# Pair pipelines for the softmax attentions of a three-block transformer kernel: order of heads, product blocks and side work

## What is computed

```python
# first block: attentions
oa = softmax(qa @ ka.T * scale + rel_bias, causal) @ va          # 8 heads of 64
ob = stick_breaking(qb, kb, vb)                                  # 8 heads of 64
mixed = (g_a * (oa @ w_br_moba) + g_b * (ob @ w_br_sb)) @ w_out
# even block
w = p[:, :, 0] - lam * p[:, :, 1]; o_a = rmsnorm(w @ a_v, subln) * 0.8
idx = top_k(sum_h relu(i_q @ i_k.T) * i_w, 64)                   # per query
o_b = softmax over the selected keys (b_q @ b_k.T) @ b_v
x = x + rmsnorm(concat(o_a, o_b) @ even_w_out, g[3])
# odd block: two groups of 8 heads
o = softmax(q @ k.T * scale + bias, chunks <= own) @ v
x = x + rmsnorm(o @ odd_w_out, g[3])
```

## Time and profile before

| | us |
|---|---|
| median of three runs | 1498.01 (1497.97 to 1501.21) |
| the profiled execution | 1496.0 |
| its span | 1494.2 |
| PE busy in the span | 1420.8 |
| DVE busy | 894.2 |
| ACT busy | 748.2 |

### The profile page before, as it was taken

How to read it: one execution, slowest core, us unless ns; L and a number is a source line. 1 busy time by engine, 2 the same in 40 slices (tenths; PEclk the granted TensorE clock), 3 DMA queues, 4 the chain that set the end, 5 groups by cost and what they waited for, 6 DMA issues and landing times.

```text
span 1494.2 us, 18003 instructions
## 1 busy us (share of the span) xinstructions
PE 1420.8 (95%) x6775; PEld 1167.7 (78%) x6775; DVE 894.2 (60%) x1125; ACT 748.2 (50%) x1039; POOL 82.6 (6%) x133
## 2 busy tenths in 40 slices
PE   5999998999999999998799999999999999999998
PEld 4878877778877888876577888878888778778886
DVE  5577775788775554467746655456544454665543
ACT  4557735646545434355466543445344466564442
POOL 3011100000000000031200000000000100000000
PEclk9999999999999999999799999999999999999999
DMA  9787644467553766444224855638565363465650
GB/s 355 272 301 232 204 150 163 160 235 251 199 169 121 234 195 197 146 141 143 69 85 155 281 175 192 193 104 267 184 194 177 132 209 113 133 221 198 195 169 29
DMA packets 177446, 274.29 MB, mean 184 GB/s; under 512 B 6449, under 2 KB 120881, under 8 KB 177361
## 3 DMA queue, kind: packets, MB, share of 16 engines
q1 hardware_dynamic: 170656, 250.87, 50.8%
q0 software_dynamic: 5552, 20.20, 4.3%
q10 hardware_dynamic: 1153, 2.07, 0.4%
HBM read 272.05 MB, written 1.06 MB: 183 GB/s over the span
## 4 chain that ended last, share of the span: by engine, by line
PE 68%; DVE 8%; issue 3%; ACT 3%; DMA 1%; POOL 0%; DVEq 0%; SPq 0%; POOLq 0%; ACTq 0%
PE psum L2212 21%; PE psum L2214 21%; PE psum L2213 21%; DVE w_lo L1839 2%; PE psum L2413 2%; DVE PR L2151 1%; DMA raw<-in_w_up_dram 1%; ACT w_hi L1637 1%; DVE scr L2174 1%; PE psum L2288 1%; ACT attn L1757 0%; PE psum L2342 0%; PE psum L2341 0%; PE psum L2357 0%; DVE lo_qk L1839 0%
## 5 line engine op out<-in xcount | busy, mean ns | idle before, releaser
L1839 DVE TENSOR_TENSOR w_lo<-raw,w_hi 128x2048 fp32r<-128x2048 f32 (+1 forms) x158 | 358.6, 2273 | 213.0 <-ACT w_hi L1637 212.6
L2212 PE MATMUL psum<-w_hi,hT_hi 128*128 128x512 f32 x1000 | 400.9, 401 | 19.7 <-DVE w_lo L1839 8.5
L2214 PE MATMUL psum<-w_hi,hT_lo 128*128 128x512 f32 x1000 | 392.0, 392 | 0.0
L2213 PE MATMUL psum<-w_lo,hT_hi 128*128 128x512 f32 x1000 | 391.1, 391 | 0.0
L1637 ACT ACTIVATE w_hi<-raw 128x2048 fp32r<-128x2048 f32 (+1 forms) x158 | 300.0, 1901 | 136.6 <-PE psum L2214 92.4
L2212 PEld LDWEIGHTS psum<-w_hi,hT_hi 128*128 128x128 f32 x1000 | 189.6, 190 | 64.8 <-issue 17.5
L2214 PEld LDWEIGHTS psum<-w_hi,hT_lo 128*128 128x128 f32 x1000 | 189.0, 189 | 40.5
L2213 PEld LDWEIGHTS psum<-w_lo,hT_hi 128*128 128x128 f32 x1000 | 189.6, 190 | 37.0 <-issue 0.5
L1839 DVE TENSOR_TENSOR lo_qk<-raw,hi_qk 128x2048 fp32r<-128x2048 f32 (+1 forms) x35 | 79.3, 2264 | 41.5 <-ACT hi_qk L1637 41.5
L2212 PE MATMUL psum<-w_hi,hc_hi 128*128 128x512 f32 x256 | 101.0, 395 | 1.8 <-DVE hc_lo L1844 1.1
L1839 DVE TENSOR_TENSOR lo_at<-raw,hi_at 128x2048 fp32r<-128x2048 f32 x35 | 80.1, 2290 | 34.8 <-ACT hi_at L1637 34.7
(11 more groups left out here) (207 smaller groups left out, 2014.2 us busy)
## 6 DMA issues: line engine op xcount, KB each, us to landing
raw<-in_ffn_wg_dram SPq DMA_DIRECT2D x88, 512.0 KB, 4.0
raw<-in_ffn_wu_dram SPq DMA_DIRECT2D x88, 512.0 KB, 5.0
raw<-in_ffn_wd_dram SPq DMA_DIRECT2D x44, 1024.0 KB, 4.9
raw<-in_w_up_dram SPq DMA_DIRECT2D x44, 512.0 KB, 5.0
raw<-in_w_in_dram SPq DMA_DIRECT2D x19, 1024.0 KB, 7.7
ada_raw<-in_w_ada_dram POOLq DMA_DIRECT2D x24, 512.0 KB, 5.2
raw<-in_even_w_in_dram SPq DMA_DIRECT2D x12, 1024.0 KB, 5.1
raw<-in_odd_w_in_dram SPq DMA_DIRECT2D x12, 1024.0 KB, 5.2
```

The costliest lines, as they stand in the source:

```text
L1839: nc.vector.tensor_tensor(lo_of(s), raw_of(s), hi_of(s).bitcast(F32), ALU.subtract).then_inc(lo_ready, 1)
L2212: nc.tensor.matmul(o, a_hi, b_hi, start=start, stop=False)
L2213: nc.tensor.matmul(o, a_hi, b_lo, start=False, stop=False)
L2214: return nc.tensor.matmul(o, a_lo, b_hi, start=False, stop=stop)
```

## The change

- `softmax_heads` is replaced by `attention` (a record of one attention) and `softmax_pairs`, which runs one or several attentions as one pipeline of pairs with three stages: in step i the scores and exponentials of pair i, the `probturn` of pair i-1 and the `pv` of pair i-2. In the last step `pv` of the pair before last and `probturn` of the last come first, then the fillers, then `pv` of the last. Each step has four places for fillers: ahead (before the scores), dense (before `exp`), late (after it), end.
- First block: one block a step (qb, qb, kb, kb, vb), one quarter a step, in the late place; the head turns of qb and kb move to steps 3 and 4 and to banks 2 and 3; after the last step come two more quarters, the second block of vb, and sums. The five quarters of `fb` stay where they are. `projout` is apart from the block.
- Even block: top-k round 0 comes ahead of the attention, the others after the splits of a step; bq's turn ahead of the block in step 3; bk's turn and `diffout` of token tile 0 after the first attention; block 5 second half in two halves around the first scores of the second attention, whose steps 1 to 3 have no block until `out_first` at the end of step 3.
- Odd block: one pipeline of eight pairs; the evacuation of the first group falls in step 5.
- `out_second`, the first half block of the second output half, moves from `out_rest` (after the last `pv`) to the last step (before it), with the splits of two further units.
- `diffout` is made by token tile.

Core of the diff:

```diff
...
+    def softmax_pairs(groups, fills):
+
+
+        pairs = [(g, j) for g in groups for j in range(4)]
+        n = len(pairs)
+
+        def qk(g, j):
+            for h in (2 * j, 2 * j + 1):
+                pl.add("qk", n=g["n0"] + h, h=h, base=g["base"], bias=g["bias"],
+                       use=pl.use(4 + h % 2, read_by=("logits_ready", g["n0"] + h + 1)), ready=g["q_ready"](h))
+
+        def exp(g, j):
+            for h in (2 * j, 2 * j + 1):
+                pl.add("exp", n=g["n0"] + h)
+
+        def probturn(g, j):
+            for h in (2 * j + 1,) if g["diff"] else (2 * j, 2 * j + 1):
+                k = n_turned_heads[0]
+                n_turned_heads[0] += 1
+                use = pl.use(2 + k % 2)
+                pl.add("probturn", n=g["n0"] + h, k=k, use=use, diff=g["diff"])
+                g["kt"][h] = k, use
+
+        def pv(g, j):
+            for h in (2 * j + 1,) if g["diff"] else (2 * j, 2 * j + 1):
+                first = g["o"] is None
+                if first:
+                    g["o"] = [pl.use(0), pl.use(1)]
+                slot = j if g["diff"] else h
+                k, turned = g["kt"][h]
+                pl.add("pv", n=g["n0"] + h, k=k, turned=turned, slot=slot, v=g["v_col"] + slot * g["v_w"], w=g["v_w"],
+                       uses=g["o"], first=first, last=h == 7, v_ready=g["v_ready"]())
+            if j == 3 and g["done"]:
+                g["done"](g)
+
+        for i in range(n + 1):
+            here = dict(zip(("ahead", "dense", "late", "end"), fills[i] if i < len(fills) else ()))
+
+            def filler(name):
+                for f in here.get(name, ()):
                     f()
 
-        for j in range(4 + 1):
-            this, before = (2 * j, 2 * j + 1), (2 * j - 2, 2 * j - 1)
-            if j < 4:
-                for h in this:
-                    pl.add("qk", n=n0 + h, h=h, base=base, bias=bias,
-                           use=pl.use(4 + (n0 + h) % 2, read_by=("logits_ready", n0 + h + 1)),
-                           ready=q_ready(h))
-            if diff and j:
-                pl.add("mix", n=n0 + before[1])
-            filler()
-            if j:
-                pend_v += [(h, t_of(h)) for h in (before[1:] if diff else before)]
-            if j < 4:
-                for h in this:
-                    pl.add("exp", n=n0 + h)
-            filler()
-            while pend_v:
-                pv(*pend_v.pop(0))
-        while fill:
-            filler()
-        return n0, state["o"]
+            filler("ahead")
+            if i < n:
+                qk(*pairs[i])
+            if i and pairs[i - 1][0]["diff"]:
+                pl.add("mix", n=pairs[i - 1][0]["n0"] + 2 * pairs[i - 1][1] + 1)
+            if i == n:
+                pv(*pairs[i - 2])
+                probturn(*pairs[i - 1])
+            filler("dense")
+            if i < n:
+                exp(*pairs[i])
+            filler("late")
+            if i == n:
+                pv(*pairs[i - 1])
+            else:
+                if i >= 2:
+                    pv(*pairs[i - 2])
+                if i:
+                    probturn(*pairs[i - 1])
+            filler("end")
...
-    def turn_second():
-        turns_of("qb", 3, 8, 6, ("uses", r["qb"]))
-        turns_of("kb", 4, 12, 6, ("uses", r["kb"]))
-
-    fa = [[sum_next, quarter, f] for name in ("qb", "kb", "vb") for f in heads_of[name]]
-    fa += [[sum_next, turn_second], [quarter], [sum_next]]
+    def turn_qb():
+        turns_of("qb", 3, 8, 2, ("uses", r["qb"]))
+
+    def turn_kb():
+        turns_of("kb", 4, 12, 2, ("uses", r["kb"]))
+
+    qb, kb, vb = heads_of["qb"], heads_of["kb"], heads_of["vb"]
+    fa = [((), [sum_next, qb[0]], [quarter]),
+          ((), [sum_next, qb[1]], [quarter, qb[2]]),
+          ((), [sum_next, kb[0]], [quarter]),
+          ((), [sum_next, turn_qb, kb[1]], [quarter, kb[2]]),
+          ((), [sum_next, turn_kb, vb[0]], [quarter], [sum_next, quarter, vb[3], sum_next, quarter, sum_next])]
 
     gates = [chunk_fillers(f"gate{i}", 6 + i, (0, BANK, 3 * BANK, 4 * BANK)[i], "tanh") for i in range(4)]
-    n0, o = softmax_heads(fa, "moba", 2 * BANK, HD, q_ready_of("qa", "ka"), lambda: r["va"])
+    moba = attention("moba", 2 * BANK, HD, q_ready_of("qa", "ka"), lambda: r["va"],
+                     done=lambda g: o_evac(g["o"], ("scr", 0), False, g["n0"]))
+    softmax_pairs([moba], fa)
...
+        def out_second(w):
+            def go():
+                outs[1] = [pl.use(2), pl.use(3, by_unit=True)]
+                outs["p"] = out_unit(w, 1, 0)
+                pl.split_to(outs["p"]["unit"] + 2)
+                product_step("proj", outs["p"], ts=(0,), inc=None)
+            return go
+
         def out_rest(src, w, chain, head):
-            outs[1] = [pl.use(2), pl.use(3, by_unit=True)]
-            p = out_unit(w, 1, 0)
+            p = outs["p"]
             pl.gate[p["unit"] + 3] = pl.gate[p["unit"] + 4] = n_scr[0]
-            product_step("proj", p, ts=(0,), inc=None)
...
+            topk(0)[0]()
             sd = pl.new_stat(8)
+
+            def diff_out(t):
+                return lambda: pl.add("diffout", t=t, uses=diff["o"], st=sd, n0=diff["n0"])
 
             def diff_var():
                 sd["n"] = pl.var()
+                pl.add("diffvar", uses=diff["o"], st=sd, n=sd["n"])
 
             def diff_norm(t):
                 return lambda: pl.add("diffnorm", t=t, st=sd, n=sd["n"])
 
+            diff = attention("mask", 2 * BANK, 2 * HD, q_ready_of("aq", "ak"), lambda: u2, diff=True)
+            fills = [((), [first_of(3)], topk(1, 2)),
+                     ((), [second_of], [finish] + topk(3)),
+                     ((), [first_of(4)], topk(4) + [rope_of(3, "bq")]),
+                     ((), [turn_of(3, "bq", 8), second_of], [finish] + topk(5, 6)),
+                     ((), [first_of(5)], topk(7) + [rope_of(4, "bk")])]
+            softmax_pairs([diff], fills)
+            turn_of(4, "bk", 12)()
+            diff_out(0)()
+            sel = attention("sel", 5 * BANK, HD, q_ready_of("bq", "bk"), lambda: held[5], base=8,
+                            done=lambda g: o_evac(g["o"], ("scr", BANK), True, g["n0"]))
+            fills = [([half_of((0, 1), None)], [half_of((2, 3), "unit")], [diff_out(1), finish]),
+                     ((), (), [diff_var]),
+                     ((), (), [lambda: diff_norm(0)(), lambda: diff_norm(1)()]),
+                     ((), (), [lambda: turn_first("scr", ("scr_ready", scr_version()))()], [out_first(W["even_w_out"][0])]),
+                     ((), [out_second(W["even_w_out"][0])])]
+            softmax_pairs([sel], fills)
...
+            fills = [((), [odd_first(1)]),
+                     ((), [odd_second], [finish]),
+                     ((), [odd_first(3)]),
+                     ((), [turn_of(1, "pq", 8), odd_second], [finish]),
+                     ([odd_start(5, (0,)), turn_of(3, "pk", 12), odd_go_on((1,), None)], [odd_go_on((2, 3), "unit")]),
+                     ((), [odd_second], [finish]),
+                     ((), (), (), [lambda: turn_first("pr", ("uses", first["o"]))()]),
+                     ((), [out_first(W["odd_w_out"][0])]),
+                     ((), [out_second(W["odd_w_out"][0])])]
+            softmax_pairs([first, second], fills)
```

More of the change, by code:

```diff
@@ L402, in head_turn, with attention @@
         return use
[L404 removed]
+    def attention(bias, v_col, v_w, q_ready, v_ready, diff=False, base=0, done=None):
         n0 = n_attn[0]
         n_attn[0] += 8
[L409 to L455 removed]
@@ L932, in branch @@
         return uses, part
[L934 removed]
+    moba_out, ya, yb, y = moba["o"], {}, {}, []
     GM, GW = {}, {}
@@ L1178, in build_plan, with finish, topk @@
+            def finish():
+                pl.add("projout", ts=(0, 1), **held["parts"][1])
+            def topk(*js):
+                return [lambda j=j: pl.add("topk", j=j) for j in js]
+            topk(0)[0]()
             sd = pl.new_stat(8)
-            pl.add("diffout", uses=o, st=sd, n0=n0)
-            v = scr_version()
+            def diff_out(t):
+                return lambda: pl.add("diffout", t=t, uses=diff["o"], st=sd, n0=diff["n0"])
             def diff_var():
                 sd["n"] = pl.var()
-                pl.add("diffvar", uses=o_diff, st=sd, n=sd["n"])
+                pl.add("diffvar", uses=diff["o"], st=sd, n=sd["n"])
@@ new lines, in odd_go_on, with finish, turn_of @@
+            def odd_go_on(ks, inc):
+                return lambda: product_step("proj", uo["parts"][0], ks=ks, inc=inc)
+            def odd_second():
+                add_products(uo["parts"][1])
+            def finish():
+                pl.add("projout", ts=(0, 1), **uo["parts"][1])
+            def turn_of(i, nm, blk):
+                return lambda: turns_of(nm, i, blk, 2, ("uses", uo[i]))
+            first = attention("odd0", 4 * BANK, HD, q_ready_of("oq", "ok"), lambda: uo[4],
+                              done=lambda g: o_evac(g["o"], ("pr", 0), False, g["n0"]))
```

(29 more changed lines are left out.)

85 lines of the change are left out of this document (31 added, 54 removed).

## The result

| | before | after |
|---|---|---|
| median | 1497.99 us | 1519.74 us (1517.97 to 1525.28, four runs) |
| ratio to before | | 1.0149, 95% interval 1.0118 to 1.0181 |
| span of the profiled execution | 1494.2 | 1517.4 |

A forecast was written before the change was run, and what follows sets the result against it. TensorE (PE) is 95% busy, so only its idle and half-clock time in the attentions can be won. +10.1 - 7.9 + 0.9 = +3.1 on 1496.0 gives 1499.1, with 2.0 for the median 1501.1 us; range 1490.5 to 1508.5.

The forecast's parts named there:

- First block, +10.1 forecast: First block into stick-breaking: late quarters shift the last adasum by +8.2 us, and the low clock adds +1.9.
- the four sums: adasum 4 to 7 on PE, fed by DVE's quarters; the last was to wait from 134.4 until 140.9.
- 4.7 to 5.7: Bounds in us for a landing, the reload of a quarter's half buffer from POOL's issue to DVE's use; 5.3 used.
- Rival B: First blocks: same quarter chain, but the last three landings nearer 7 than 5.3 us; slower, 1505.6 to 1508; chance 0.33.
- the walk: The prediction's step-by-step timing of the new order, block 5.56 us each; adasum 7 shifts +8.2, even block's last turn -9.4.
- +1.9 by that row: Stick-breaking: clock cost of the 6.5 us gap before adasum 7, taken from the old block after the 4.75 gap.
- about 3 us more: High end if the stick-breaking gap and the even block's bare stretch both fall to 1.2 GHz: about 3 us above the sum.
- Even block, -7.9 forecast: Even block: last turn 9.4 us earlier, the 0.86 split wait gone, less 2.4 of low clock; bounds -12 and -4.
- 0 and 5: Bounds in us on the low-clock cost where the even block's PE has only small work and gaps; 2.4 taken.
- rival D: Even block gains nothing, since the last mix and rope stay late and the clock low: +10, 1508; chance 0.05.
- Tails and odd block, +0.9 forecast: Odd block: new gaps of 4.0 us against old 2.2 and the 0.9 split wait; bounds -1 and +2.5.
- Splits stay as they are: DVE's weight splits beside POOL's work keep their length, 2.35 against 2.29 us, though the mix stretches.

The follow-up runs named there:

- even_scores_first: The changed kernel with the first half of block 5b and its split moved behind the first scores of the even block's second attention; ratio to before 1.0113.
- even_v2: The changed kernel with its even block reordered: top-k rounds and bq's turn later, block 5a in halves, block 5b behind the scores; ratio to before 1.0086.
- best: The kernel before with the even block in even_v2's order and the odd block as changed, first block as before; ratio to before 0.9940.
- best_old_odd: The kernel best with the odd block's old attention calls put back; ratio to before 0.9926.

## Why the prediction was wrong

**First block, +10.1 forecast, +17.6 measured (at the even block's first scores).** The mechanism was right: one quarter a step behind the splits, then the full cycle. The waits before the four sums were forecast as 2.1, 0.5, 2.5 and 6.5 and are 3.8, 0.6, 2.6 and 5.3, 12.3 against 11.6; the total is nearer than its parts. Quarter 4 came at 123.3 instead of near 117. Quarter 1's landing of 7.7 was outside my 4.7 to 5.7: I had seen one of 7.5 and left it out of the bounds. Rival B wanted the last three landings near 7; one of them was (quarter 7's 6.7; quarter 5's was 5.4, the halves of quarter 6 took 4.4 and 5.6), so B names the sign but not the cause of the excess. The idle time grew by 10.7 where the walk had 8.2. The term that failed is "+1.9 by that row" for the clock: the busy time grew by 7.0. I had priced one drop behind the longest gap; with the waits of 3.77, 2.61 and 5.31 the clock fell each time, and parts of the blocks behind them and two of the sums themselves (2.05 for 1.10, 1.84 for 1.02) ran at half speed. The trace of before could have told me, for its half clock was not only behind the gap of 4.75 that I read, but also at the two other waits for the mix:

```profile
735.47 0.87 PE L2357 MATMUL psum<-cst,attn 128*128 128x128 f32 x3 [3.52 <-DVE attn L2030]
...
741.59 0.87 PE L2357 MATMUL psum<-cst,attn 128*128 128x128 f32 x3 [3.02 <-DVE attn L2030]
...
734.50:745.00 10.50, 5.93 (x26) 5.30 (x26) 6.77 (x22) 4.13 (x14) 0.28 (x1) 0.51 0.01 2
```

The Trainium skill ("TensorE: Matmul & The Clock Gate", section "Why this matters for your kernels") wants no long idle gaps between bursts; I had used it for "about 3 us more" at the high end. The trace agrees for the waits of 3.77 and 5.31, shows the same behind 2.61, and makes the price 7.0 here.

**Even block, -7.9 forecast (-7.0 of it inside the stretch), +3.0 measured there** (the wait of 0.86 behind it, went as forecast, but half clock behind the 1.99 wait took its place). The prediction had named a stretch that shrinks by less than 4 as the sign that it is wrong. The step that failed is the walk itself. Its waits sum to 1.7 + 3.1 + 4.1 + 1.1 + 2.1 + 0.4 = 12.5, against 14.5 idle before: of the 9.4 us gain only 2 was waiting. The other 7.4 lay in reckoning every block at 5.56 and every small piece at its full-speed length, though PE's busy time before was 71.95 at a clock of 0.88. I had booked the return of the clock without saying so, and charged 3.1 (0.7 and 2.4) for what would stay. What the low clock cost can be estimated as half of PE's busy time at 0.50: 7 before (3.3, 4.7 and 5.9 us busy in its three low stretches), nearly all of the 7.4, and 9 in the change (18 us busy). So it didn't return but cost more: 0.88 again, with 13.7 us at 0.50 in the bare stretch, about 5.2 by the same estimate, where I had 2.4 and bounds of "0 and 5". The idle time was short by 2.9: 1.1 more at bq's turn, 0.6 more at the mix, and two waits I had at nothing, 1.22 at bk's turn and 1.44 at the scores. The last is a queue I didn't walk: on DVE the split issued with block 5b's first half stands ahead of the read of the scores. even_scores_first and even_v2 show that both the waits and the clock hang on those places: E 85.1 and 78.0. So rival D's mechanism (mix and rope late, clock low) is what came, and at 0.05 I had given it far too little: nothing in the walk excluded it. (Its price was also too low by my own terms: without the even block's gain the sum is 10.1 + 0.9 = +11.0, which is 1509, above the range.)

**Tails and odd block, +0.9 forecast, +1.5 and 0.6 behind.** Right within its bounds: the evacuation waits are 1.99 both times (2.1 forecast). The traces of best and best_old_odd, 1.6 and 0.6, agree.

**Contention.** "Splits stay as they are" was wrong as a rule, though it cost the forecast nothing: the change's splits did not meet POOL (2.28 at 732.00, after POOL's last at 730.42 had ended). The row I took it from the earlier trace rows shows a split of 2.35 beside POOL, and two POOL operations of 4.57 together, where 1.3 each is usual: there POOL paid. In even_scores_first the split paid:

```profile
733.79 3.38 DVE L1920 TENSOR_TENSOR w_lo<-raw,w_hi 128x2048 fp32r<-128x2048 f32 x1
```

So the Trainium skill ("GPSIMD Engine Reference", section 8, Key points), which has POOL contend with DVE instructions of two SBUF inputs, holds for the split as well: the trace agrees, with 3.38 against 2.29. I had noted this as a possibility, with each rope's add 1 to 2 us later.

## What to carry to other kernels

When you walk a new order at full-speed lengths, compare PE's busy time and clock in the old stretch with the sum of your walk first: the difference is a gain you are booking for the clock, and here it came only where the waits were closed (69.3 us busy in even_v2, 74.0 in the change). Look at every wait in the old trace that the clock fell behind, not only at the longest. A step that is moved takes its split with it in every queue, and a score read or a bank's read behind it is then late: write out DVE's and ACT's queues from the first to the last step, not only around the moved ones. A chain through one buffer that reloads after use has a fixed cycle, and once late it stays late; a consumer moved back only finds the next thing that the same producer holds up.

## What the hardware showed that was not expected

- In the change PE's clock went to half at waits of 1.99 to 5.31 us, and in a stretch of small matmuls broken by waits it stayed there for 13.7 us. `adasum` of eight matmuls took 1.84 instead of 1.02.
- The length of a wait did not decide it. The same wait of 1.99 before the even block's last turn was followed by half clock in the change and not in best_old_odd; one of 2.65 (even_scores_first, 739.88) and one of 3.04 (there, 91.86) were not either. A drop or its absence in one trace is thus partly luck, worth some 1.7 us of PE time at the last turn (half of the 3.30 us at 801.50). What else decides it was not tried. best_old_odd:

```profile
775.54 1.06 PE L2429 MATMUL psum<-cst,scr 128*128 128x128 f32 x8 [1.99 <-DVE scr L2189]
...
775.54:780.00 4.46, 4.46 (x24) 3.71 (x25) 2.16 (x3) 3.80 (x4) 0.00 (x0) 1.00 0.67 231
```

- Beside POOL's rope a DVE operation on 128x2 took 1.40 us instead of 0.22, and the two mixes 2.79 instead of 0.75:

```profile
727.85 1.40 DVE L2108 SCALAR_TENSOR_TENSOR rsum<-rsum,lam,sums 128x2 f32<-128x2 f32 x1
...
729.28 2.79 DVE L2111 SCALAR_TENSOR_TENSOR attn<-attn,rsum 128x128 f32<-128x128 f32 x2
```

- Which side of that contention pays differs: once POOL (4.57 for two operations that take 1.3 each in the even block's attentions), once the split (3.38 for 2.29).
- Landings of the same reload, issue to use with DVE waiting, were 5.4 (124.89 to 130.25), 6.7 and 7.7 in one execution. What makes them differ was not tried.
